# The low halves of the expert weights made by VectorE instead of GpSimd, in a decoder layer with 16384 single-neuron experts

## The reference, cut to what matters

```python
def peer(x, w_q, sub_keys, u_tab, v_tab):       # u_tab, v_tab: 16384 x 2048
    ...
        q = (xb @ w_q).reshape(TOKEN_BLOCK, PEER_HEADS, 2, PEER_HALF)
        s = jnp.einsum('thcd,hcnd->thcn', q, sub_keys)
        vals, idx = lax.top_k(s, PEER_TOPK)
        ...                                     # ids: 8 heads x 16 experts a token, g: softmax of their scores
        h = jax.nn.gelu(jnp.einsum('td,thkd->thk', xb, u_tab[ids]))
        w = g * h
        return jnp.einsum('thk,thkd->td', w, v_tab[ids])
```

## Time and profile before

| | us |
|---|---|
| median of 3 runs | 4197.86 |
| lowest and highest | 4195.37, 4198.47 |
| the profiled execution, span from its first to its last instruction | 4197.0 |

### The profile page before, as it was taken

The page is one execution under the profiler, slowest core; times in us unless marked ns, Lnnn a source line. Parts: engine busy times, 40 slices in busy tenths (PEclk is TensorE's granted clock), DMA queues, the critical chain, the costliest instruction groups (busy, mean ns, idle before and its releaser), DMA issues.

```text
span 4197.0 us, 58676 instructions
## 1 busy us (share of the span) xinstructions
PE 3930.4 (94%) x20049; PEld 3581.4 (85%) x20049; DVE 2771.7 (66%) x3434; ACT 1423.0 (34%) x2272; POOL 2439.8 (58%) x1056
## 2 busy tenths in 40 slices
PE   8999999989998999899899899989989899898999
PEld 7777777768886899899899899979989899898777
DVE  4555555534314997967967967468888888888642
ACT  4333333341114223544544644312222222222342
POOL 4343333334443455777777777767767677676633
PEclk9999999999999999999999999999999999999999
DMA  4222222224433233688788687866767767677322
GB/s 153 92 87 87 87 87 90 94 84 140 153 122 117 89 120 145 226 310 300 255 305 300 259 302 299 315 245 253 275 257 271 273 253 273 256 271 269 150 85 85
DMA packets 206054, 822.51 MB, mean 196 GB/s; under 512 B 16944, under 2 KB 107184, under 8 KB 118576
## 3 DMA queue, kind: packets, MB, share of 16 engines
q1 hardware_dynamic: 137648, 515.62, 34.6%
q0 software_dynamic: 36864, 268.45, 16.3%
q10 hardware_dynamic: 31488, 37.76, 2.5%
HBM read 754.66 MB, written 67.11 MB: 196 GB/s over the span
## 4 chain that ended last, share of the span: by engine, by line
PE 45%; DVE 26%; issue 12%; POOL 10%; DVEq 4%; ACT 1%; ACTq 1%; DMA 1%; POOLq 0%; SPq 0%
PE bank L604 14%; PE bank L606 14%; PE bank L605 14%; DVE yacc L1602 8%; POOL wlo L568 7%; DVE sc L1339 6%; DVE wt L1585 5%; POOL urows L585 3%; DVEq L1596 2%; DVE xwhi L1589 1%; DVE res L1635 1%; PE bank L647 1%; DVE urows L1536 1%; DVE xwlo L1591 1%; PE bank L666 1%
## 5 line engine op out<-in xcount | busy, mean ns | idle before, releaser
L568 POOL TENSOR_TENSOR wlo<-raw,whi 128x1024 fp32r<-128x1024 f32 x788 | 2062.4, 2621 | 1691.9 <-ACT whi L990 1643.8
L990 ACT ACTIVATE whi<-raw 128x1024 fp32r<-128x1024 f32 x784 | 827.5, 1059 | 2391.9 <-PE bank L606 2034.1
L604 PE MATMUL bank<-ahi,whi 128*128 128x384 f32 (+1 forms) x3968 | 1465.8, 369 | 29.6 <-DVE alo L1288 8.0
L605 PE MATMUL bank<-alo,whi 128*128 128x384 f32 (+1 forms) x3968 | 1449.4, 365 | 0.0
L606 PE MATMUL bank<-ahi,wlo 128*128 128x384 f32 (+1 forms) x3968 | 1449.1, 365 | 0.0
L604 PEld LDWEIGHTS bank<-ahi,whi 128*128 128x128 f32 x3968 | 758.5, 191 | 124.8 <-issue 36.1
L606 PEld LDWEIGHTS bank<-ahi,wlo 128*128 128x128 f32 x3968 | 756.4, 191 | 78.6
L605 PEld LDWEIGHTS bank<-alo,whi 128*128 128x128 f32 x3968 | 758.0, 191 | 73.0 <-issue 0.5
L604 PE MATMUL bank<-xwhi,whi 128*128 128x384 f32 x2048 | 705.2, 344 | 97.4 <-DVE xwlo L1591 87.2
L605 PE MATMUL bank<-xwlo,whi 128*128 128x384 f32 x2048 | 701.3, 342 | 0.0
L606 PE MATMUL bank<-xwhi,wlo 128*128 128x384 f32 x2048 | 701.0, 342 | 0.0
(11 more groups left out here) (204 smaller groups left out, 2819.1 us busy)
## 6 DMA issues: line engine op xcount, KB each, us to landing
raw<-ws SPq DMA_DIRECT2D x394, 1024.0 KB, 4.9
gelu_spill<-hst ACTq DMA_DIRECT2D x128, 192.0 KB, 1.9
route_spill<-gst SPq DMA_DIRECT2D x24, 1024.0 KB, 11.6
hg<-gelu_spill SPq DMA_DIRECT2D x64, 384.0 KB, 7.9
hg<-route_spill SPq DMA_DIRECT2D x64, 384.0 KB, 8.6
gate_spill<-gout ACTq DMA_DIRECT2D x32, 256.0 KB, 2.1
gl<-gate_spill SPq DMA_DIRECT2D x32, 256.0 KB, 2.8
xin<-xT SPq DMA_DIRECT2D x8, 512.0 KB, 8.3
```

Of the source, the lines that this page charges most:

```text
L568: nc.gpsimd.tensor_tensor(wlo[:, s], raw[:, s // 2, s % 2], whi[:, s].bitcast(F32), ALU.subtract).then_inc(lo_done, 1)
L604: pe.matmul(ps_out, hi, xh, start=first, stop=False)
L605: pe.matmul(ps_out, hi, xl, start=False, stop=False)
L990: act.activation(whi[:, s], raw[:, s // 2, s % 2], ACT.Copy).then_inc(hi_done, 1)
```

## The change

POOL makes the low parts only up to block `DVE_LO` (the first block of the routing tiles) and again from `B7` on, behind the expert stages. In between it issues the 256 gathers alone. DVE makes the 472 low parts between, two blocks ahead of the iteration of the tile (`LEAD`), and one ahead of and one behind each pair's evacuation in stage 6. The 20 dots of a tile move: 4 in its first 16 blocks, 16 in its other 16. ACT, PE and SP are as before.

```diff
+NTG = 20
+TILE_DOTS = [j % 4 == 3 or j >= 16 for j in range(32)]
+POST_DOTS = [j % 2 == 0 and j < 16 for j in range(4 * (64 - POST))]
+LEAD = 2
+DVE_LO = B5 + 4 * PRE
...
-            lo_parts(0, B5 + 4 * PRE)
-            with pool.Fori(0, NRT) as t:
-                with_gathers(32 * t + (B5 + 4 * PRE), NTG * t, TILE_GATHERS, u_tab, urows)
-            with_gathers(B5 + 4 * POST, NTG * NRT, POST_GATHERS, u_tab, urows)
-            with_gathers(B6, NP, GROUP0_GATHERS, v_tab, vrows)
-            with pool.Fori(1, 16) as g:
-                with_gathers(16 * g + B6, 8 * g + NP, GROUP_GATHERS, v_tab, vrows)
+            def gather_rows(first, table, rows):
+                for n in range(NP):
+                    s = n % RING
+                    pool.wait_ge(idx_ok, first + n + 1)
+                    nc.gpsimd.indirect_dma_start(
+                        rows[:, s], None, table,
+                        bass.IndirectOffsetOnAxis(ap=idxs[:, s, 0:1], axis=0)).then_inc(rows_in[s], 16)
+
+            lo_parts(0, DVE_LO)
+            gather_rows(0, u_tab, urows)
+            gather_rows(NP, v_tab, vrows)
+            pool.wait_ge(lo_done, B7)
             lo_parts(B7, NB - B7)
...
+            def lo_part(b, s):
+                dve.wait_ge(hi_done, b + 1)
+                dve.tensor_tensor(wlo[:, s], raw[:, s // 2, s % 2], whi[:, s].bitcast(F32),
+                                  ALU.subtract).then_inc(lo_done, 1)
...
-                for g in range(GT):
-                    if g == 2:
+                for j, with_dot in enumerate(TILE_DOTS):
+                    lo_part(32 * t + (DVE_LO + LEAD + j), (j + LEAD) % 4)
+                    if j == 2:
                         if first:
                             dve.wait_ge(x1_out, 64)
                         else:
                             dve.wait_ge(tile_out, t * 64)
-                    if g >= 2:
-                        take_group(t, g - 2)
-                    one_hots(GT * t + g, g % 2)
-                    if g % 4 != 0:
+                    if 2 <= j < GT + 2:
+                        take_group(t, j - 2)
+                    if j < GT:
+                        one_hots(GT * t + j, j % 2)
+                    if with_dot:
                         next_dot()
-                for g in range(GT - 2, GT):
-                    take_group(t, g)
-                    next_dot()
-                while n < NTG:
-                    next_dot()
...
+            dve.wait_ge(lo_done, DVE_LO)
+            for j in range(LEAD):
+                lo_part(DVE_LO + j, j)
             routing_tile(0, first=True)
...
-            for n in range(NTG * NRT, NP):
-                dot(n, n // RING, n % RING, more=n + RING < NP)
+            n = NTG * NRT
+            for j, with_dot in enumerate(POST_DOTS):
+                if B5 + 4 * POST + LEAD + j < B6:
+                    lo_part(B5 + 4 * POST + LEAD + j, (j + LEAD) % 4)
+                if with_dot:
+                    dot(n, n // RING, n % RING, more=n + RING < NP)
+                    n += 1
...
             for k in range(8):
                 expert_weights(0, k, 0)
+                if k >= 5:
+                    lo_part(B6 + k - 5, k - 5)
+            lo_part(B6 + 3, 3)
...
                 for u in range(8):
+                    ahead = not last or u < 6
                     if not last:
                         expert_weights(g + 1, u, 1 - q)
+                    if ahead:
+                        lo_part(g * 16 + (B6 + 2 * u + 4), 2 * u % 4)
                     dve.wait_ge(blk_done, g * 16 + (B6 + 2 * u + 2))
...
                         add_rows(8 * g + u, 2 * g + u // RING, u % RING, more=not (last and u >= RING))
+                    if ahead:
+                        lo_part(g * 16 + (B6 + 2 * u + 5), (2 * u + 1) % 4)
```

More of the change, by code:

```diff
@@ L78 @@
 RING = 4
[L80 to L85, removed]
+NTG = 20
+TILE_DOTS = [j % 4 == 3 or j >= 16 for j in range(32)]
+POST_DOTS = [j % 2 == 0 and j < 16 for j in range(4 * (64 - POST))]
+assert sum(TILE_DOTS) == NTG and NTG * NRT + sum(POST_DOTS) == NP and NTG % RING == 0
+LEAD = 2
+DVE_LO = B5 + 4 * PRE
 C_BIAS, C_LNG, C_LNB, C_SLOPE, NCPAR = W, W + 1, W + 2, W + 3, W + 5
```

## The result

| | before | changed |
|---|---|---|
| median, us | 4198.16 (4 runs) | 4311.57 (4 runs) |
| lowest, highest | 4195.37, 4203.27 | 4305.68, 4315.29 |
| profiled execution: its own time, its span | its span 4197.0 | 4312.01, 4310.2 |

The ratio is 1.0267, 95% interval 1.0252 to 1.0281: slower, by 113 us. Forecast was 4255 in a range of 4185 to 4320: the time lies in the range, and the cost of 113 us is twice the 57 that the sum gave.

What follows compares the result with a forecast made beforehand. DVE was taken to bound a tile's first half and the value stage, PE the second half. Terms 105 + 14 - 2 - 63 + 3 = +57 on a span of 4197.0, plus 0.9 for the median: 4255 us, range 4185 to 4320.

Steps and rivals of the forecast that it cites:

- the ring of waits: First half of a tile: scaling, high part, low part, reduction, one-hots run in series, 7.24 us a round; +18.4 a tile.
- Value stage: Groups 1 to 14: quiet DVE, but every second pair waits for `hg`; 70.5 us a group instead of 75.0, -63.
- Seam and group 0: Behind the tiles: PE dense, value stage starting 6 us late, first group 66.6 plus some 8 instead of 87; together -2.
- Last group: Last value group: DVE needs about 9.6 us a pair, 1.3 over PE, for six pairs, delaying the end; +3.
- Second half: Second half of a tile: 16 gathers instead of 8, DVE a few us behind, next tile's one-hots late; +2.6 a tile.
- Covered by the ring: POOL's gathers: 2.8 us for most indirect DMAs, covered by four slots that leave 16 us; costs nothing.
- B: Value stage: `hg` lands by 8.6 us after the low part, not 9.65, PE never stops; -118, 4200 us; chance 0.17.
- C: First half of a tile: neighbouring links overlap more, shorter round; faster only under 6.4 us a round; chance 0.08.
- D: Value stage gains nothing or loses: `hg` lands 1 us later, 74.4 us a group, -8, 4310 us; chance 0.13.
- E, the clock: First half of a tile: repeated short PE idle times halve the clock, rounds average perhaps 7.8 us; +45, 4300; chance 0.12.

Runs made afterwards that it cites:

- Experiment 1: Changed kernel with the reduction and one-hots of a group ahead of DVE's low part in a routing tile, not behind it: 4106.05 us, ratio to before 0.9778.
- experiment 2: Changed kernel with the pair's second low part ahead of the weighted addition in the value stage, not behind it: 4252.22 us, ratio to before 1.0127.
- experiment 4: Changed kernel with ACT's gelu waiting for the spill of its own slot, not the other slot's just issued: 4267.20 us, ratio to before 1.0162.
- experiment 7: Changed kernel, dots still 4 and 16; one-hots before low part, pair's second low part before addition, gelu waiting for its own slot's spill: 4004.87 us.
- experiment 3: Changed kernel with a tile's dots placed 12 and 8 in its two halves instead of 4 and 16: 4252.03 us, ratio to before 1.0129.
- the gelu edit: Kernel before the change, with gelu waiting for its own slot's spill instead of the other slot's: 4197.53 us against 4198.68, ratio 0.9997.

## Why the prediction was right, and where it was off

*Direction and mechanism.* The forecast was slower, and the time is in its range, with the ring of waits as the cause: a round of 7.24 us was worked out, 7.19 measured; first to last routing 103.7 against 103.0 (103.4 in the first tile). Experiment 1 shows it as the cause: only the order differs. With the measured 64 us of the second halves in place of 13 the sum would be 108, against 113.

*Value stage.* A group was put at 70.5 us and bound by the `hg` loads; measured 70.9, with 56 waits for `hg` in 14 groups, four a group, one for every second pair. Landing stayed at 8.3. Experiment 2 shows the link. The term was -63, measured -54.9: the groups are 0.5 us longer than forecast and were 0.1 shorter before than the 75.0 I took.

*Seam and group 0.* -2 forecast; +12.5 and -12.2 measured, +0.3. Of the 12.5 us, 4.7 are PE's longer wait at the start of the value stage (6.6 instead of 1.9), which I had put at 6; the other 7.8 lie in the blocks before it, 6.0 of them in the 16 behind the sixth tile's last routing, which the sum left out with "PE is dense and stays so". That the term came out so near is in part luck.

*Last group.* +3 forecast, -2.8 measured. The lag of DVE that I had reckoned with does not show: in experiment 2, where PE does not wait at this group's start, the group takes 66.7 us, PE's own time. With the change it takes 68.4 and before 69.7, after idle times of 3.1 and 5.5 us, with granted clocks of 0.58 and 0.50 in the 4 us behind them. The other 1.5 us lie behind the value stage, in stages that the change's diff leaves alone; their cause stays open.

*The step that failed* is "Second half": I put 70 to 74 us of DMA time into 67, concluded that "DVE falls a few us behind" and wrote +2.6 a tile for "the next tile's one-hots start late". The measured term is +12.7, 64 us in all where the term had 13, and that difference is most of the 56 us by which the sum fell short. DVE wasn't the one who suffered: its dots' waits for rows are 35 us in the whole run, and the next tile's one-hots were ready 5.6 us before ACT scaled them. I looked only at what the gathers' own readers do, and not at who else waits on the DMA engines with an order of its own. ACT's gelu waits for its last spill, ACT's scaling stands behind that gelu, and PE waits for both. The load was low too: the half held 81 us of DMA time (0.95 over 85.6 us), and 74 to 75 where the gelu's wait is gone (experiments 4 and 7). Experiments 3 and 4 show both halves, the crowd and the wait.

*Indirect DMAs.* "Covered by the ring" held. They took 1.40 us in the mean for u rows, 1.70 for v rows (1.63 and 1.30 before), not the 2.8 that I took for most, and the rows were hardly waited for. A gather beside a low part on DVE, first DVE and then POOL:

```profile
3429.07 1.23 DVE L1526 TENSOR_TENSOR wlo<-raw,whi 128x1024 fp32r<-128x1024 f32 x1
```

```profile
3429.38 1.72 POOL L583 DMA_INDIRECT vrows<-v_tab,idxs  x1 [6.10 <-DVE idxs L1531]
```

The 17 gathers that ran beside no DVE instruction took 0.94 us. This one took 0.78 us more, and the low part had 0.92 us to run when it began.

*Rivals.* B needed `hg` a us earlier; that came only by experiment 2's edit. C needed a round under 6.4 us (7.1 with B), D a landing later than 8.3; neither came. E, the clock, came halfway: with an idle time of 2.0 to 2.3 us in most rounds the granted clock of a first half fell to 0.93 in the mean, but it cost nothing. Two rounds of that tile (length, busy, clock, DMA share, GB/s):

```profile
1932.10:1939.30 7.20, 5.11 (x23) 0.78 0.34 137
...
1946.50:1953.70 7.20, 4.93 (x30) 1.00 0.07 27
```

The routings in and around both windows are 7.18 to 7.20 us apart, at 0.78 as at 1.00: PE had the slack.

## What to carry to other kernels

When work moves to an engine that runs in order, write down one round of every loop of semaphores that its new wait closes, link by link with measured durations, and compare the round with the bound engine's period; where the new work stands relative to what others wait for matters more than its length. Do the same for every wait on a DMA whose landing time will grow: a wait that costs nothing at 7.8 us of 8.3 costs at 10.1, and most where the next loop's first link stands behind it (7.8 us at each tile's start). A change that loses as a whole can hold a gain: with three places in the order and one semaphore put right, this one ends 219 us below the kernel before. (How far the kernel before would come with orders of its own was not tried, but for the gelu edit, which gives it nothing.)

## What the runs showed of the hardware that I had not expected

The clock behind short idle times is not decided by their length alone. In the value stage of the changed kernel, an idle time of 2.53 us was followed by a clock of 0.58 (levels of 1.2 and 2.4 GHz mixed in the window), and a longer one of 2.68 us left it at full (the two waits, then windows of 4 us behind them: length, busy, clock, DMA share, GB/s):

```profile
3495.34 0.44 PE L599 MATMUL bank<-xwhi,whi 128*128 128x384 f32 x1 [2.53 <-DVE xwlo L1598]
```

```profile
3920.95 0.44 PE L599 MATMUL bank<-xwhi,whi 128*128 128x384 f32 x1 [2.68 <-DVE xwlo L1598]
```

```profile
3495.40:3499.40 4.00, 4.00 (x14) 0.58 0.96 399
3920.95:3924.95 4.00, 4.00 (x23) 1.00 0.97 401
```

Idle times of 4.12 us (3281.83) and 1.86 us (3210.87) were followed by 0.50 and 1.00. What separates the two in the middle I can't say from these rows. And the spill of 192 KB by ACT's queue lands in 1.9 us in the median, but in 9.4 where two other queues fill the DMA engines to 0.94. SP's loads of 1 MB landed in 9.6 us in the median there (4.8 in the first half): a small transfer took about as long as a large one.
